# Sparse attention in a two-block transformer kernel: key root mean square and index key deviation taken by tokens, and spread over the rows by matmuls

## What is computed

```python
q = _rope(_rmsnorm(q, q_norm_g), positions)
k = _rope(_rmsnorm(k, k_norm_g), positions)
qi = _rope(qi, positions)
ki = _rope(_layernorm(ki, idx_k_ln_g, idx_k_ln_b)[:, :, None, :], positions)[:, :, 0, :]
...
score = jnp.einsum('bqhs,bqh->bqs', jax.nn.relu(s), wib).astype(jnp.float32)
_, sel = lax.top_k(score, topk)
```

## Time and profile before

| | us |
|---|---|
| median of 3 runs | 2729.09 |
| lowest, highest | 2725.72, 2729.58 |
| the profiled execution's own time | 2730.6 |
| its span | 2728.8 |
| TensorE busy | 2666.2 |
| VectorE busy | 1311.9 |
| ScalarE busy | 920.8 |
| GpSimd busy | 761.0 |

### The profile page before, as it was taken

How to read it: one execution, slowest core, us unless ns; L and a number is a source line. 1 busy time by engine, 2 the same in 40 slices (tenths; PEclk the granted TensorE clock), 3 DMA queues, 4 the chain that set the end, 5 groups by cost and what they waited for, 6 DMA issues and landing times.

```text
span 2728.8 us, 30557 instructions
## 1 busy us (share of the span) xinstructions
PE 2666.2 (98%) x12622; PEld 2172.7 (80%) x12626; DVE 1311.9 (48%) x1861; ACT 920.8 (34%) x1517; POOL 761.0 (28%) x628
## 2 busy tenths in 40 slices
PE   8999999999999999999999998999999999999999
PEld 7878887777777778888788666788888888888887
DVE  4344256566565544534524598463332554633323
ACT  4222234333344322422224344642222332422221
POOL 6563025564444567076700241000000000000000
PEclk9999999999999999999999998999999999999999
DMA  6554245443333354354433120133333323433332
GB/s 174 160 147 122 95 118 139 111 129 106 92 105 100 96 166 149 100 148 144 145 125 103 47 62 1 63 85 93 100 101 131 101 85 93 128 96 96 97 116 77
DMA packets 382379, 296.49 MB, mean 109 GB/s; under 512 B 15588, under 2 KB 335328, under 8 KB 382208
## 3 DMA queue, kind: packets, MB, share of 16 engines
q1 hardware_dynamic: 363632, 240.33, 29.8%
q0 software_dynamic: 17072, 52.64, 6.5%
q10 hardware_dynamic: 1536, 1.58, 0.2%
HBM read 290.79 MB, written 2.13 MB: 107 GB/s over the span
## 4 chain that ended last, share of the span: by engine, by line
PE 86%; DVE 8%; ACT 3%; POOL 1%; DMA 1%; issue 1%; SPq 0%; DVEq 0%; ACTq 0%; POOLq 0%
PE PS L410 18%; PE PS L411 17%; PE PS L413 15%; PE PS L488 7%; PE PS L490 7%; PE PS L489 7%; PE PS L415 2%; PE PS L447 1%; PE PS L449 1%; PE PS L448 1%; PE PS L940 1%; DVE WL L1651 1%; DVE SETS L1660 1%; PE PS L725 1%; PE PS L912 1%; ACT SETS L1031 1%
## 5 line engine op out<-in xcount | busy, mean ns | idle before, releaser
L410 PE MATMUL PS<-HH,WH 128*128 128x512 f32 x2248 | 901.3, 401 | 0.1
L411 PE MATMUL PS<-HL,WH 128*128 128x512 f32 x2248 | 878.9, 391 | 0.0
L413 PE MATMUL PS<-HH,WL 128*128 128x512 f32 x1967 | 769.4, 391 | 0.0
L1651 DVE TENSOR_TENSOR WL<-RAW,WH 128x1024 fp32r<-128x1024 f32 (+1 forms) x306 | 403.9, 1322 | 552.5 <-ACT WH L1031 552.0
L410 PEld LDWEIGHTS PS<-HH,WH 128*128 128x128 f32 x2248 | 424.7, 189 | 111.8 <-issue 26.8
L411 PEld LDWEIGHTS PS<-HL,WH 128*128 128x128 f32 x2248 | 424.7, 189 | 89.9 <-issue 5.5
L1031 ACT ACTIVATE WH<-RAW 128x1024 fp32r<-128x1024 f32 (+1 forms) x318 | 330.2, 1040 | 360.9 <-PE PS L415 301.8
L413 PEld LDWEIGHTS PS<-HH,WL 128*128 128x128 f32 x1967 | 371.3, 189 | 79.0
L2504 POOL TENSOR_SCALAR ADA<-ADA,CA 128x512 f32<-128x512 f32 x168 | 297.4, 1770 | 10.4 <-DMA ADA<-in_ada_w 2.8
L2501 POOL TENSOR_TENSOR ASUM<-ASUM,ADA 128x512 f32<-128x512 f32 x168 | 228.8, 1362 | 14.0
L1651 DVE TENSOR_TENSOR WLr<-RAWD,WHr 128x1024 fp32r<-128x1024 f32 x82 | 101.4, 1238 | 258.0 <-ACT WHr L1031 258.0
(11 more groups left out here) (358 smaller groups left out, 3280.8 us busy)
## 6 DMA issues: line engine op xcount, KB each, us to landing
ADA<-in_ada_w POOLq DMA_DIRECT2D x192, 256.0 KB, 3.2
RAW<-in_ffn_w_gate SPq DMA_DIRECT2D x88, 512.0 KB, 3.9
RAW<-in_ffn_w_up SPq DMA_DIRECT2D x88, 512.0 KB, 3.9
RAWD<-in_ffn_w_down SPq DMA_DIRECT2D x88, 512.0 KB, 3.5
RAW<-in_w_in SPq DMA_DIRECT2D x84, 512.0 KB, 4.0
RAW<-in_conv_w_in SPq DMA_DIRECT2D x24, 512.0 KB, 3.8
RAW<-in_attn_w_in SPq DMA_DIRECT2D x16, 512.0 KB, 3.8
RAW<-in_w_mlstm_branch SPq DMA_DIRECT2D x8, 512.0 KB, 4.1
```

The costliest lines, as they stand in the source:

```text
L410: pe.matmul(PS[:, b, :], wh[:, k, :], hi[:, k, :], start=k == 0, stop=False)
L411: pe.matmul(PS[:, b, :], wh[:, k, :], lo[:, k, :], start=False, stop=False)
L413: pe.matmul(PS[:, b, :], wl[:, k, :], hi[:, k, :], start=False, stop=False)
L1651: return v.tensor_tensor(out, x, y, op).then_inc(*tick("dve", *event))
```

## The change

The sums of squares are taken as for the queries, by tokens: four matmuls with the squares as the stationary operand give one column (index key) or two (key tiles) for each 128 tokens, on all 128 partitions. ScalarE's root and VectorE's reciprocal then work on 4 or 8 columns of SM, in place. Two turns later, in a further PSUM bank, matmuls with the column repeated 64 times as the stationary operand and the identity as the moving one spread the reciprocals over the rows: 4 for the index key, 8 for each key tile (two heads by four token blocks). VectorE multiplies the key with that bank directly. The number of yields is kept in the key tiles and grows by one in the index key.

```diff
--- before.py
+++ after.py
@@ -348,6 +348,12 @@
     return m["F17"][:, (2 * p + e) % 8, 0:W], m["F16"][:, (2 * p + e) % 4, 0:W]
 
 
+def key_rms(m, c):
+
+
+    return m["SM"][:, 60 + 8 * c:60 + 8 * c + (8, 8, 4)[c]]
+
+
 def least(m, p, e):
 
     c = 32 + (2 * p + e) % 12
@@ -833,11 +839,24 @@
         b = yield from behind.bank()
         w.wait_ge(*at("ki sq"))
         clear(b)
-        pe.matmul(PS[0:64, b, :], B, s2[0:64, :], start=True, stop=True).then_inc(*tick("pe", "ki var"))
+        for tb in range(4):
+            ins = pe.matmul(PS[:, b, tb:tb + 1], s2[0:64, tb * P:(tb + 1) * P], B64[0:64, 0:1], start=True, stop=True)
+        ins.then_inc(*tick("pe", "ki var"))
         free[b] = ("ki std",)
         behind.leave(b)
-        for _ in range(3):
-            yield
+        yield
+        yield
+        b = yield from behind.bank()
+        w.wait_ge(*at("ki root"))
+        clear(b)
+        rms = key_rms(m, 2)
+        for tb in range(4):
+            ins = pe.matmul(PS[0:64, b, tb * P:(tb + 1) * P], rms[:, tb:tb + 1].to_broadcast([P, 64]), ident, start=True, stop=True)
+        ins.then_inc(*tick("pe", "ki rms"))
+        free[b] = ("ki scaled",)
+        yield
+        behind.leave(b)
+        yield
         yield from rope(j, ("ki n",), ("ki",), 64)
         known.add("ki2")
 
@@ -877,12 +896,27 @@
         b = yield from behind.bank()
         w.wait_ge(*at("s2", "k", c))
         clear(b)
-        pe.matmul(PS[:, b, :], B64, s2, start=True, stop=True).then_inc(*tick("pe", "kv", c))
+        for tb in range(4):
+            ins = pe.matmul(PS[:, b, 2 * tb:2 * tb + 2], s2[:, tb * P:(tb + 1) * P], B64[:, 0:P:64], start=True, stop=True)
+        ins.then_inc(*tick("pe", "kv", c))
         free[b] = ("k std", c)
         yield
         behind.leave(b)
         yield
-        for _ in range(5):
+        yield
+        b = yield from behind.bank()
+        w.wait_ge(*at("k root", c))
+        clear(b)
+        rms = key_rms(m, c)
+        for tb in range(4):
+            for e in range(2):
+                ins = pe.matmul(PS[64 * e:64 * e + 64, b, tb * P:(tb + 1) * P],
+                                rms[:, 2 * tb + e:2 * tb + e + 1].to_broadcast([P, 64]), ident, start=True, stop=True)
+        ins.then_inc(*tick("pe", "k rms", c))
+        free[b] = ("k n", c)
+        yield
+        behind.leave(b)
+        for _ in range(3):
             yield
         yield from rope(j, ("k n", c), ("k", c))
 
@@ -1459,10 +1493,14 @@
             yield
         b = yield from behind.bank()
         w.wait_ge(*at("ki var"))
-        act(s2, PS[0:64, b, :], ACT.Sqrt, "ki std", bias=eps[0:64], scale=1.0 / 64.0)
-        behind.leave(b)
-        for _ in range(3):
-            yield
+        act(key_rms(m, 2), PS[:, b, 0:4], ACT.Sqrt, "ki std", bias=eps, scale=1.0 / 64.0)
+        behind.leave(b)
+        yield
+        yield
+        b = yield from behind.bank()
+        yield
+        behind.leave(b)
+        yield
         yield from rope(j, ("ki",))
         known.add("ki2")
 
@@ -1501,10 +1539,14 @@
         b = yield from behind.bank()
         yield
         w.wait_ge(*at("kv", c))
-        act(s2, PS[:, b, :], ACT.Sqrt, "k std", c, bias=eps, scale=1.0 / 64.0)
-        behind.leave(b)
-        yield
-        for _ in range(5):
+        act(key_rms(m, c), PS[:, b, 0:8], ACT.Sqrt, "k std", c, bias=eps, scale=1.0 / 64.0)
+        behind.leave(b)
+        yield
+        yield
+        b = yield from behind.bank()
+        yield
+        behind.leave(b)
+        for _ in range(3):
             yield
         yield from rope(j, ("k", c))
         for _ in range(4):
@@ -2246,19 +2288,23 @@
         behind.leave(b)
         known.add("wi")
         yield
-        s2 = take_s2()[0:64, :]
+        take_s2()
         for _ in range(2):
             yield
         b = yield from behind.bank()
         behind.leave(b)
         w.wait_ge(*at("ki std"))
-        recip(s2, s2)
-        done()
-        tt(x, x, s2, ALU.mult)
+        recip(key_rms(m, 2), key_rms(m, 2), "ki root")
+        yield
+        yield
+        b = yield from behind.bank()
+        yield
+        w.wait_ge(*at("ki rms"))
+        tt(x, x, PS[0:64, b, :], ALU.mult, "ki scaled")
+        behind.leave(b)
         done()
         ts(x, x, vec(m, "idx_k_ln_g_2")[0:64], vec(m, "idx_k_ln_b_2")[0:64], ALU.mult, ALU.add, "ki n")
-        for _ in range(3):
-            yield
+        yield
         yield from rope(j, KI[0:64, :], ("ki",), 64)
         done()
         copy(KI[64:128, :], KI[0:64, :], "ki twice")
@@ -2345,17 +2391,23 @@
         yield from rope(j, QT[:, c, :], ("q", c))
 
     def k_tile(c, j):
-        s2, x, kt = take_s2(), xs[j], KT[:, c, :]
+        take_s2()
+        x, kt = xs[j], KT[:, c, :]
         yield
         b = yield from behind.bank()
         yield
         behind.leave(b)
         yield
         w.wait_ge(*at("k std", c))
-        recip(s2, s2)
-        done()
-        tt(x, x, s2, ALU.mult, "k n", c)
-        for _ in range(5):
+        recip(key_rms(m, c), key_rms(m, c), "k root", c)
+        yield
+        yield
+        b = yield from behind.bank()
+        yield
+        w.wait_ge(*at("k rms", c))
+        tt(x, x, PS[:, b, :], ALU.mult, "k n", c)
+        behind.leave(b)
+        for _ in range(3):
             yield
         yield from rope(j, kt, ("k", c))
```

## The result

The changed kernel took 2734.90 us (median of 17 runs, 2727.54 to 2737.62) against 2729.09 us for the kernel before in the same comparison (17 runs, 2724.85 to 2731.34). The ratio is 1.0022, 95% interval 1.0015 to 1.0029: about 6 us slower, where 5.7 us less were forecast. The profiled execution took 2733.96 us with a span of 2732.2. Three of the 17 times lie at 2727.5 to 2729.4 us and the other 14 at 2732.4 or more; the three profiles taken of this kernel are all of the upper group.

The account below looks back on a forecast made before the run. TensorE bounds the kernel, busy 2666.2 of 2728.8 us; VectorE savings count only where TensorE idles for them. 0.3 + 1.6 + 0.8 + 3.0 = 5.7 us gained, from 2729.09 to 2723.4 us; range 2719.5 to 2729.5.

Parts of the forecast that it names:

- Sums by tokens, roots, reciprocals: Index key and key tiles: sums and roots change nothing; each of three reciprocals 3.1 us less, second key's scaling 0.69 us.
- Spreading matmuls: New TensorE work, 4 + 8 + 8 matmuls: 4.3 us plus 0.5 for changes of stationary width, 4.8 us added.
- rival (d): Key-tile halves overlap, narrow matmuls cost like transposes, or no bank wait: gain of 6.7 to 9.6 us; chance 0.22.
- Index key: Last index query's rotation: wait falls to about 0.8 us, 0.3 us gained, and 1.6 us from the higher clock behind it.
- TensorE in the key tiles: Up to the fourth query's rotation: 3.8 us of spreading plus 1.0 of wait less 1.3 of old wait, 3.5 us later.
- The bank wait: First query's rotation must wait 1.0 us until VectorE has read the first key's spread reciprocals from the PSUM bank.
- no wait under 1.78 us shows it: Argument that TensorE's clock stays high behind shorter waits, used against the low clock staying.
- The second gap: TensorE's 4.85 us wait before the first probabilities' transposes falls to 0.6 us; transposes start earlier, 0.8 us gained.
- the 3.0 us for the clock: Behind the first transposes' wait: 6.76 busy us at clock 0.52 run at full clock instead, 3.0 us gained.
- After that scores come in time for both engines: Behind the first transposes and their clock gain: no further waiting for scores, no further term in the sum.
- (b): Wait at the first query's rotation is long: 2.5 us with low clock, gain 1.2, or slower; chance 0.17, 0.07 slower.
- (a): Low clock stays at one or both old places: 1.6 or 3.0 us less, gain 4.1, 2.7 or 1.1; chance 0.17.

Follow-up runs that it names:

- the two rounds less: Changed kernel with two of 16 rounds of maximum and replacement left out for one token block on VectorE, so other keys are chosen: 0.9997 to the kernel before.
- the late version: Changed kernel with the first query's rotation one turn later on all engines: 0.9978 to the kernel before, 2723.75 us.
- the fillers: Matmuls nobody reads, placed in TensorE's waits; three in the changed kernel with the first query's rotation one turn later: 0.9971 to the kernel before, 2721.6 us.
- the version with the moved product: Changed kernel with the low part of one weight chunk moved from GpSimd to VectorE, behind the first scores: 1.0008 to the kernel before.
- the kernel before with fillers: Kernel before the change plus three matmuls nobody reads in TensorE's waits, nothing else: 0.9986 to the kernel before.

## Why the prediction was wrong

*Sums by tokens, roots, reciprocals.* Right. The reciprocals of SM take 0.18 and 0.19 us (forecast 0.2 to 0.34), and both key scalings, with a PSUM operand, 0.68.

*Spreading matmuls.* Too dear. With 0.216 us each and 0.17 for each group, 4.8 us were forecast; the first index score behind each group came 1.1 and 1.2 us late, and the index key's group takes about as long, so 3.4 us. A key tile's eight matmuls take the 1.09 us of the index key's four. That is rival (d), and what the Trainium skill says in "TensorEngine Tiling (Array Packing)", section "Key Properties", of tiles that work in parallel; the trace agrees as far as the two heads' halves cost no more than one.

*Index key.* Right at its own place, and in part by luck: 0.3 + 1.6 us forecast, 1.6 measured, less 0.05. The wait is 0.96 against 0.8, with no half clock behind it, and VectorE's rows show the order that was forecast: reciprocal early, scaling held by the spreading matmuls for 1.21 us, the add still with its unexplained 0.46 us:

```profile
1530.84 0.18 DVE L1708 RECIPROCAL SM<-SM 128x4 f32<-128x4 f32 x1 [3.09 <-ACT SM L1065]
...
1535.37 0.68 DVE L1693 TENSOR_TENSOR TS<-TS,PS 64x512 f32<-64x512 f32 x1 [1.21 <-PE PS L854]
...
1539.09 0.68 DVE L1693 TENSOR_TENSOR KI<-KI,TS 64x512 f32<-64x512 f32 x1 [0.46 <-DVE TS L1693]
```

The 1.6 us are what the half clock behind the 1.78 us wait had cost in the kernel before. Of seven profiles with that wait (1.78 or 1.79 us) the clock fell behind it in four, both of the kernel before among them, and held in three. So the gain is not there in every execution, and in the profile of the index key's part alone it was lost again, as shown above.

*TensorE in the key tiles.* 3.5 us forecast, 3.8 measured, but made of other things: 1.5 us less for spreading, and 1.65 us of half clock that had been put at nothing. The bank wait itself was exact, 1.0 against 0.99. What failed is the sentence "no wait under 1.78 us shows it", behind which stood "behind the waits of 1.27 and 1.41 us the following matmuls keep the full rate". Two or three rows of one profile were taken for a rule about the length of a wait. Behind 0.99 us the clock fell in six of eight profiles, all three of the changed kernel among them, and held in those of the key tiles alone and of the two rounds less. And the 1.41 us wait itself is in the changed kernel followed by the 20.5 us at half clock.

*The second gap.* This is the step that turned the result: "VectorE, 7.6 us lighter, now waits for it; it takes the result at 1628.5 instead of 1629.23", and "The 8.9 us from there to the first scores stay". VectorE took it at 1628.80, and on the prediction's scale, where the index key's 4.2 us are put back, at 1633.0, so 4.5 us late. The 7.6 us were not saved but stood idle and held. VectorE reached the end of its work at 1595.80 and idled 4.68 us, for scores that TensorE could not deliver behind the bank wait and at half clock (3.06 us where the clock held, 1.03 in the late version, without the bank wait). Then GpSimd's products caught it at 1607.08 and 1616.19, 2.2 and 2.0 us over what these instructions take alone, and twice more, as before the change:

```profile
1624.81 2.08 DVE L1651 TENSOR_TENSOR QT<-QT,TS 128x512 f32<-128x512 f32 x1
...
1631.81 3.27 DVE L2318 TENSOR_TENSOR_SCAN SCW<-TS 128x512 f32<-128x512 f32 x1
```

Once it is held, VectorE's own work no longer decides when the first scores come: in all ten profiles in which the scan takes 3.27 or 3.28 us, of the kernel before, the changed kernel and each half alone among others, the wait is 4.79 to 4.85 us, whatever work VectorE had. The prediction had used this very effect for one scaling, and treated every other SBUF instruction as if its length were its own. By the first transposes the key tiles were to gain 0.8 us; they lost 3.8, all that TensorE had taken on. That is 4.6 us of error, the largest in the sum. Of the 3.0 us for the clock 0.9 came.

*After that scores come in time for both engines.* Wrong, and nearly as large: 4.3 us lost behind 1667 us, where "no stretch at 0.52" was the test that the prediction set itself. Why the stretch is so long in the changed kernel stays open; the fillers show only that idle gaps have a part in it. Of the rivals, (b) names the place of the bank wait but asked for a longer wait; (a) is nearest, but counted only the old low stretches as staying, not a longer one. The chance of slower, 0.04, was far too small. It came from one mechanism's far end, although the profile showed three separate stretches at half clock, each with an idle gap of TensorE ahead of it (1.78, 4.85 and 2.37 us).

## What to carry to other kernels

Instructions of VectorE with two SBUF inputs took 0.48 to 1.23 us alone and 2.1 to 3.3 beside GpSimd's products, so GpSimd's schedule sets their length: before crediting work saved on VectorE, ask whether it moves VectorE past GpSimd's next product, since a lead that doesn't reach it is taken away again (2.9 us less work gave 6.8 us, 7.6 us less gave none). A turn in a ring of buffers that is added for a small result may make an unrelated step wait; moving that step one turn was worth 12 us here, though it cost 3 us in the kernel before. Where TensorE must wait in short gaps, harmless matmuls in them can keep its clock; they gave 6 us in the changed kernel. And a clock that fell or held in one profile is one draw: before counting on it, look at a second.

## What the runs showed of the hardware

The granted clock does not follow the length of a wait alone. Behind the same wait at the same place it differs from profile to profile: behind 0.99 us it fell in six of eight profiles (in the changed kernel to 0.62 over 4.5 us), behind 1.78 or 1.79 us in four of seven, behind 1.24 to 1.27 us in two of four. Behind the 0.96 us wait it held in all eleven. Where it fell in the stretch of short matmuls behind 1667 us, it stayed at 1.2 GHz for 20.5 us in the changed kernel although TensorE was busy for 19.02 of them, and in the kernel before for 6.8 us with more idle time. In the four versions with three fillers 3.5 us of that stretch or nothing was left, so idle gaps have a part in starting it. What ends it, and why its length repeats so exactly in each kernel (20.5 us three times, 6.8 us twice), was not settled; the waits ahead of it are not enough, for behind the kernel before's two waits of 1.41 and 2.37 us the version with two rounds less had 13.8 us (0.50 over 1665.25 to 1679.00).

A small scaling (128x32, one SBUF input) took 1.03 instead of 0.18 us beside GpSimd's product at 1632.07 in the version with the moved product, and 1.06 beside that at 1625.06 in the kernel before with fillers, so not only instructions with two inputs are held.
